# Modulation in two column halves, with six projection tiles begun between them

## The reference, cut to what matters

```python
c_act = silu(c)                                   # [1, 1024]
mod = c_act @ w_ada + b_ada                       # [1, 3072]
shift, scale, gate = split(mod, 3)
u = layer_norm(x) * (1 + scale) + shift           # [512, 1024]
proj = u @ w_in + b_in                            # [512, 12288]
a_v, a_g, b_b, b_c, b_h, b_g, c_a, c_b, c_g, merge = split(proj, ...)
... # pooling (a), short convolution (b), 31-tap convolution of c_a * sigmoid(c_b) (c)
m = sum over i of sigmoid(merge_i) * (y_i @ w_branch[i])
x = layer_norm(ALPHA * x + gate * (m @ w_out), ln_g, ln_b)
... # second block: two layers of attention, gates and a feed-forward part
```

## Time and profile before

| | |
|---|---|
| median of three runs | 2192.2 us |
| the profiled execution's own time | 2193.3 us |
| its span | 2191.5 us |
| TensorE busy | 2162.6 us, 99% |
| VectorE busy | 1258.1 us, 57% |
| ScalarE busy | 770.9 us, 35% |
| granted TensorE clock, mean | 0.996 |

### The profile page before, as it was taken

How to read it: one execution, slowest core, us unless ns; L and a number is a source line. 1 busy time by engine, 2 the same in 40 slices (tenths; PEclk the granted TensorE clock), 3 DMA queues, 4 the chain that set the end, 5 groups by cost and what they waited for, 6 DMA issues and landing times.

```text
span 2191.5 us, 25652 instructions
## 1 busy us (share of the span) xinstructions
PE 2162.6 (99%) x10739; PEld 1798.8 (82%) x10739; DVE 1258.1 (57%) x1617; ACT 770.9 (35%) x1019; POOL 24.9 (1%) x42
## 2 busy tenths in 40 slices
PE   6999999999999999999999999999999999999998
PEld 3888888888888888988888888889898888888887
DVE  7899797944656847434765554234743476555422
ACT  2323232323343354344353333135434434333311
POOL 1000000000000100000000000000000000000000
PEclk9999999999999999999999999999999999999999
DMA  9432232332233322322223233222232222323322
GB/s 318 137 116 82 96 101 82 99 112 96 96 101 101 103 71 77 111 77 78 96 77 99 94 105 103 91 78 89 76 114 77 77 96 78 98 95 102 107 90 77
DMA packets 184151, 217.90 MB, mean 99 GB/s; under 512 B 3805, under 2 KB 159077, under 8 KB 184037
## 3 DMA queue, kind: packets, MB, share of 16 engines
q1 hardware_dynamic: 180048, 210.52, 28.8%
q10 hardware_dynamic: 3252, 3.60, 0.5%
q0 software_dynamic: 736, 2.15, 0.3%
HBM read 212.06 MB, written 4.19 MB: 99 GB/s over the span
## 4 chain that ended last, share of the span: by engine, by line
PE 95%; DVE 1%; SPq 1%; ACT 1%; DMA 1%; issue 0%; POOL 0%; POOLq 0%; ACTq 0%; DVEq 0%
PE psum L1684 30%; PE psum L1686 30%; PE psum L1685 30%; PE psum L1974 1%; SPq L609 1%; PE psum L2005 1%; PE psum L2037 1%; DMA raw<-in_w_in 1%; PE psum L2017 1%; DVE hT L1385 0%; DVE whl L498 0%; PE psum L1961 0%; PE psum L1990 0%; ACT hT L825 0%; PE psum L1708 0%
## 5 line engine op out<-in xcount | busy, mean ns | idle before, releaser
L1684 PE MATMUL psum<-hT,whl 128*128 128x512 f32 (+1 forms) x2112 | 803.0, 380 | 7.0 <-DVE hT L1385 3.6
L1685 PE MATMUL psum<-hT,whl 128*128 128x512 f32 (+1 forms) x2112 | 796.5, 377 | 0.0
L1686 PE MATMUL psum<-hT,whl 128*128 128x512 f32 (+1 forms) x2112 | 796.4, 377 | 0.0
L498 DVE TENSOR_TENSOR whl<-raw,whl 128x1024 fp32r<-128x1024 f32 (+1 forms) x364 | 442.1, 1216 | 447.9 <-ACT whl L491 447.7
L491 ACT ACTIVATE whl<-raw 128x1024 fp32r<-128x1024 f32 (+1 forms) x364 | 380.0, 1047 | 447.3 <-PE psum L1686 429.2
L1684 PEld LDWEIGHTS psum<-hT,whl 128*128 128x128 f32 x2112 | 398.7, 189 | 87.7 <-issue 9.6
L1686 PEld LDWEIGHTS psum<-hT,whl 128*128 128x128 f32 x2112 | 398.7, 189 | 73.6
L1685 PEld LDWEIGHTS psum<-hT,whl 128*128 128x128 f32 x2112 | 399.0, 189 | 71.5 <-issue 0.5
L1684 PE MATMUL psum<-whl,ff 128*128 128x512 f32 x352 | 137.1, 390 | 0.0
L1686 PE MATMUL psum<-whl,ff 128*128 128x512 f32 x352 | 136.9, 389 | 0.0
L1685 PE MATMUL psum<-whl,ff 128*128 128x512 f32 x352 | 136.9, 389 | 0.0
(11 more groups left out here) (285 smaller groups left out, 2140.2 us busy)
## 6 DMA issues: line engine op xcount, KB each, us to landing
raw<-in_w_in SPq DMA_DIRECT2D x88, 1024.0 KB, 5.0
raw<-in_w_up SPq DMA_DIRECT2D x44, 1024.0 KB, 5.0
raw<-in_w_down SPq DMA_DIRECT2D x20, 1024.0 KB, 5.0
ada<-in_w_ada SPq DMA_DIRECT2D x12, 1024.0 KB, 13.7
raw<-in_w_branch SPq DMA_DIRECT2D x12, 1024.0 KB, 5.2
raw<-in_w_out SPq DMA_DIRECT2D x12, 1024.0 KB, 5.0
x<-in_x SPq DMA_DIRECT2D x4, 512.0 KB, 6.1
v_by_token<-vnat ACTq DMA_DIRECT2D x4, 512.0 KB, 2.9
```

The lines of the kernel that those rows point to most:

```text
L498: nc.vector.tensor_tensor(whl_view(w, 1), raw_view(w), whl_view(w, 0).bitcast(F), ALU.subtract).then_inc(w_lo, 1)
L1684: M(out_, stat_hi, mov_hi, start=start, stop=False, **kw)
L1685: M(out_, stat_hi, mov_lo, start=False, stop=False, **kw)
L1686: return M(out_, stat_lo, mov_hi, start=False, stop=stop, **kw)
```

## The change

The modulation's blocks are worked through in the order 0, 2, 1, 3: blocks 0 and 2 give shift and scale of column blocks 0 to 3, blocks 1 and 3 those of 4 to 7. `modc` is formed in two halves (`s_mod` 1 and 2). After the first half the column blocks 0 to 3 are modulated and the first six tiles (CA, CB, CG) run over contraction steps 0 to 3; between these partial tiles TensorE does the products of blocks 1 and 3; after the second half come column blocks 4 to 7 and the tiles' other four steps. Six weight tiles must lie split at once, so tiles 4 and 5 get room in the part of `ada` that block 0 has left (`room_for` waits for `s_mod` 1 there). The loads follow the new order, and the gate columns are loaded in one go after `s_mod` 2, ahead of chunk 5. Statistics start with each row block of `x`, and the normalised rows are written by ScalarE, for which VectorE prepares minus mean times the inverse deviation (`nmr`). Tiles of the first block use PSUM banks shifted by four; transposed columns use banks 0 to 3, 7, 6, 7, 6. The gate sums and the rest of the pair loops keep their places; `split_lo` and `split_hi` of tiles 3 to 5 have moved ahead of them.

```diff
-    PE_ROWS = (3, 3, 3, 5)
+    MOD_ORDER = (0, 2, 1, 3)
+    PE_ROWS = {0: 3, 2: 5, 1: 3, 3: 3}
+    X_BANK = (0, 1, 2, 3, 7, 6, 7, 6)
-            W_BANK[key] = count % 6
+            W_BANK[key] = (count + 4) % 6
+    apart.update({i: over(f"early{i}", at_ * K, [P, 2, 1024], R) for i, at_ in ((4, 0), (5, 8))})
 # room_for
+            elif w in (4, 5):
+                nc.scalar.wait_ge(s_mod, 1)
 # SP
-            for q in range(8):
-                ...
-            chunk_load(0)
-            chunk_load(1)
-            for q in range(4):
-                if q == 0:
-                    sp.wait_ge(s_mod, 1)
-                sp.dma_start(ada[:, q, :]..., wa[:, :, 2048 + q * 256:...]).then_inc(s_adag, 16)
-                chunk_load(2 + q)
-            for c in range(6, len(chunks)):
+            ada_load(0)          # two pieces each
+            ada_load(2)
+            chunk_load(0)
+            chunk_load(1)
+            ada_load(1)
+            chunk_load(2)
+            ada_load(3)
+            chunk_load(3)
+            chunk_load(4)
+            sp.wait_ge(s_mod, 2)
+            for q in range(4):
+                sp.dma_start(ada[:, 2 + q, :]..., wa[:, :, 2048 + q * 256:...]).then_inc(s_adag, 16)
+            for c in range(5, len(chunks)):
 # ScalarE
+            for tb in range(TB):
+                act.wait_ge(s_nmr, tb + 1)
+                A(xn1[:, tb, :], x[:, tb, :], ACT.Identity, bias=nmr[...], scale=rstd[...]).then_inc(s_xn, 1)
             split_hi(0)
-            split_hi(1)
-            act.dma_start(cstage[:], ...)
-            act.dma_start(gaterow, ...)
             act.wait_ge(s_modc, 1)
-            for ct in range(KT):
-                ...
+            columns_hi(0)
+            columns_hi(1)
+            split_hi(1)
+            columns_hi(2)
+            columns_hi(3)
+            for w in range(2, 6):
+                split_hi(w)
+            act.wait_ge(s_modc, 2)
+            columns_hi(4)
+            act.dma_start(cstage[:], ...)
+            act.dma_start(gaterow, ...)
+            for ct in range(5, KT):
+                columns_hi(ct)
 # VectorE: the sums in MOD_ORDER, and
-            for ct in range(0, KT, 2):
-                ...
+            ada_sum(0)
+            ada_sum(1)
+            modulation(0)
+            u_whole(0)
+            u_lo(0)
+            split_lo(0)
+            u_lo(1)
+            split_lo(1)
+            u_whole(2)
+            u_lo(2)
+            u_lo(3)
+            split_lo(2)
+            split_lo(3)
+            ada_sum(2)
+            split_lo(4)
+            split_lo(5)
+            ada_sum(3)
+            modulation(1)
+            for ct in range(4, KT, 2):
+                u_whole(ct)
+                u_lo(ct)
+                u_lo(ct + 1)
 # pair loops, ScalarE and VectorE (split_hi and split_lo alike)
-                    split_lo(W[key] + 3)
+                    if W[key] >= 3:
+                        split_lo(W[key] + 3)
 # TensorE, behind the vector transposes; part_tile(i, ks) is tile i of the first six over steps ks
             ada_product(1)
-            ...
+            take(6)
+            ada_columns(0)
+            ada_columns(1).then_inc(s_mod, 1)
+            for ct in range(4):
+                x_columns(ct)
+            part_tile(0, [0])
+            part_tile(0, [1])
+            part_tile(1, [0, 1])
+            part_tile(0, [2])
+            part_tile(1, [2])
+            part_tile(0, [3])
+            part_tile(1, [3])
+            ada_product(2)
+            part_tile(2, range(4))
+            part_tile(3, range(4))
+            ada_product(3)
+            ada_columns(2)
+            part_tile(4, range(4))
+            ada_columns(3).then_inc(s_mod, 1)
+            x_columns(4)
+            pe.wait_ge(s_modc, 2)
+            x_columns(5)
+            part_tile(5, range(4))
+            x_columns(6)
+            part_tile(0, [4])
+            x_columns(7)
+            part_tile(0, [5])
+            part_tile(1, [4])
+            part_tile(0, [6])
+            part_tile(1, [5])
+            part_tile(0, [7])
+            part_tile(1, [6, 7])
+            for i in range(2, 6):
+                part_tile(i, range(4, KT))
```

More of the change, by code:

```diff
@@ L355, in build @@
     bnst, mv, ssq, msq, rstd, neghalf = stat[:, 0:48], stat[:, 48:56], stat[:, 56:60], stat[:, 60:64], stat[:, 64:68], stat[:, 68:72]
-    modc, cact = stat[:, 72:88], stat[:, 88:96]
+    modc, cact, nmr = stat[:, 72:88], stat[:, 88:96], stat[:, 96:100]
     nmax, den = (stat[:, o_:o_ + 32].rearrange("p (k b h) -> p k b h", k=2, b=TB) for o_ in (0, 72))
@@ L371, in build @@
         w_hi, w_lo, w_used = sem("w_hi"), sem("w_lo"), sem("w_used")
-        s_x, s_vec, s_vec2, s_cst, s_cst2, s_adag, s_bcast = (sem(n) for n in ("x_in", "vec_in", "vec2_in", "cst_in", "cst2_in", "adag_in", "bcast_in"))
+        s_x = [sem(f"x_in{tb}") for tb in range(TB)]
+        s_vec, s_vec2, s_cst, s_cst2, s_adag, s_bcast = (sem(n) for n in ("vec_in", "vec2_in", "cst_in", "cst2_in", "adag_in", "bcast_in"))
         s_ada = [sem(f"ada_in{q}") for q in range(8)]
         s_c, s_cT, u_act = sem("c_in"), sem("c_transposed"), sem("u_by_act")
-        arow_ps, s_part = sem("ada_row_psum"), sem("ada_part")
+        arow_ps, s_part, s_nmr, s_xc = sem("ada_row_psum"), sem("ada_part"), sem("neg_mean_rstd"), sem("x_columns")
         s_vT, s_vcol, s_mod, s_modc, s_gp, s_gate = (sem(n) for n in ("vecT", "vcol_ready", "mod_psum", "modc_ready", "gate_psum", "gate_ready"))
@@ L670, in _ @@
             A(cact, bank(7)[:, 496:504], ACT.Silu).then_inc(s_cact, 1)
+            for tb in range(TB):
+                act.wait_ge(s_nmr, tb + 1)
+                A(xn1[:, tb, :], x[:, tb, :], ACT.Identity, bias=nmr[:, tb:tb + 1], scale=rstd[:, tb:tb + 1]).then_inc(s_xn, 1)
             act.wait_ge(s_vT, 6)
@@ L687, in _ @@
                         act.wait_ge(h_lo, ct - 1)
[L688 to L691, removed]
+                    A(utmp[:, 1, :], bank(X_BANK[ct]), ACT.Identity, bias=modc[:, ct:ct + 1], scale=modc[:, 8 + ct:9 + ct]).then_inc(u_act, 1)
+                A(hT[:, 0, ct, :], bank(X_BANK[ct]), ACT.Identity, bias=modc[:, ct:ct + 1], scale=modc[:, 8 + ct:9 + ct]).then_inc(h_hi, 1)
+            act.wait_ge(s_modc, 1)
+            columns_hi(0)
[7 more added lines that the diff above has]
+            columns_hi(4)
+            act.dma_start(cstage[:], t["consts"][:, NKEEP:NCONST]).then_inc(s_cst2, 16)
+            act.dma_start(gaterow, t["b_ada"][:, 2048:3072].to_broadcast((P, D))).then_inc(s_bcast, 16)
+            for ct in range(5, KT):
+                columns_hi(ct)
             def pair_step(p, key, j):
@@ L729, in _ @@
                     w = W[key]
-                    split_hi(w + 3)
+                    if w >= 3:
+                        split_hi(w + 3)
                     j = key[1] % 2
@@ L1054, in row_stats, with neg_mean_rstd @@
                 V.tensor_scalar(msq[:, tb:tb + 1], mv[:, 2 * tb + 1:2 * tb + 2], LN_EPS, None, ALU.add).then_inc(s_ms, 1)
-            dve.wait_ge(s_x, 16 * TB)
+            def neg_mean_rstd(tb):
+                dve.wait_ge(s_rstd, tb + 1)
+                V.tensor_scalar(nmr[:, tb:tb + 1], mv[:, 2 * tb:2 * tb + 1], rstd[:, tb:tb + 1], -1.0, ALU.mult, ALU.mult).then_inc(s_nmr, 1)
             for tb in range(TB):
+                dve.wait_ge(s_x[tb], 16)
                 half_stats(tb, 0)
@@ L1060, in _ @@
                 row_stats(tb)
[L1061 to L1064, removed]
+                if tb:
+                    neg_mean_rstd(tb - 1)
+            neg_mean_rstd(TB - 1)
             def weighted(o_, at_k, ks=range(KT)):
@@ L1075, in summed, with ada_sum @@
             def summed(g):
-                return weighted(adsum[:, 2 * g:2 * g + 2, :], lambda k: ada[:, 2 * g:2 * g + 2, k * 256:(k + 1) * 256])
+                return weighted(adsum[:, 2 * g:2 * g + 2, :], lambda k: ada[:, 2 + 2 * g:4 + 2 * g, k * 256:(k + 1) * 256])
             dve.wait_ge(s_cact, 1)
-            for b in range(TB):
+            def ada_sum(i):
+                b = MOD_ORDER[i]
                 if PE_ROWS[b] < 4:
@@ L1084, in _, with modulation @@
                 weighted(part, lambda k: ada_rows(b, k), range(PE_ROWS[b], KT)).then_inc(s_part, 1)
-                dve.wait_ge(s_part, b + 1)
-                dve.wait_ge(arow_ps, b + 1)
+                dve.wait_ge(s_part, i + 1)
+                dve.wait_ge(arow_ps, i + 1)
                 own = part[32 * b:32 * b + 1, :]
                 V.tensor_tensor(own, own, bank(7)[32 * b:32 * b + 1, :], ALU.add).then_inc(s_adsum, 1)
[L1090 to L1094, removed]
+            def modulation(h):
+                halves = lambda ap: ap.rearrange("p (a b) -> p a b", a=2)[:, :, 4 * h:4 * h + 4]
+                dve.wait_ge(s_mod, h + 1)
+                link(V.tensor_tensor(halves(modc), halves(vcol[:, VOFF["b_ada"]:VOFF["b_ada"] + 16]), halves(bank(6)[:, 0:16]), ALU.subtract))
```

(37 more changed lines are left out.)

27 lines of the change are left out of this document (12 added, 15 removed).

## The result

The changed kernel took 2200.43 us (median; 2199.13 to 2200.74), the kernel before 2192.62 in the same series: a ratio of 1.0034, 95% interval 1.0024 to 1.0045. It is 7.8 us slower, by the interval 5.3 to 9.9; the forecast was 9.1 slower, 2201.3.

What follows compares the result with a forecast made beforehand. TensorE, busy 99% of the span, was taken as the bound, with VectorE's list to the gate sum deciding this case: 6.9 us later plus 2.2 for the clock, 9.1 slower, 2201.3 us; range 2195.5 to 2206.

Steps and rivals of the forecast that it cites:

- The start: Up to tile 2: first projection at 30.35 us instead of 40.44, 5.3 us at half clock, tile 2 done at 66.9.
- the 2.8 us to spare: Block 3's modulation sum complete at 49.9 us, while TensorE wants it at 52.7.
- No gain from ten early microseconds: At tile 2 TensorE has done 36 steps at 66.9 us instead of 68.0, only 1.1 us ahead.
- What is late next: VectorE's list from tile 2 to the second gate sum ends at 99.0, 6.9 us later; TensorE waits 7.7 us.
- The clock behind the wait: After TensorE's wait for the gate sum the clock falls to half speed, costing 1.7 to 2.65 us, taken as 2.2.
- The 4.6: Price of half clock after the gate wait by the Trainium skill's reckoning, idle time counted; total loss then 11.5 us.
- The sum: Whole kernel: 6.9 us for the later gate sum plus 2.2 for the clock, 9.1 us slower.
- the two cases that it adds up: Range's upper end, 2206 us: late block 3 (2204.3 at 3 us) together with a longer half clock after the gap.
- The first (VectorE does not bind): Gate sum not binding, only the earlier start counts: 2191.1 us, or 2189 with full clock at the start; 13%.
- The full-clock start: No half clock at the first projections: tile 2 at 64.85, total 2199.2 us; 12%.
- Block 3's delay: Block 3's load, queued behind chunk 2's wait on SP, comes late and delays tile 2; 2204.3 us at 3 us; 10%.
- The longer half clock: After the gate wait the clock stays low longer, costing 4.6 us instead of 2.2: 2203.7 us; 8%.

Runs made afterwards that it cites:

- experiment 1: Changed kernel with 15 convolution items of VectorE, behind tiles CB, CB and CG of pair 0, handed out later in that pair: 2191.91 us, ratio 0.9994.
- experiment 9: Kernel before with only six idle matmuls added in TensorE's wait near 756 us: 2191.78 us, ratio 0.9996.
- experiment 6: Kernel before with 15 convolution items of pair 0 handed out later in the same pair: 2192.94 us, ratio 1.0001.
- experiment 2: Changed kernel with the gate product and VectorE's step reading it moved from behind the first AG tile to behind the first BC tile: 2198.47 us.
- experiment 5: Kernel before, start untouched, with ten convolution items of pair 0 moved ahead of the gate sums: 2201.26 us, ratio 1.0037.
- experiment 3: Changed kernel with eight idle matmuls in front of the gate product's wait: 2198.41 us, ratio 1.0026.
- experiment 4: Changed kernel with three idle matmuls between the first four column transposes and the first projection step: 2200.68 us, ratio 1.0034.

## Why the prediction was right

- *The start.* `modc` was forecast at 26.5 and came at 26.68, the first step at 30.35 and came at 30.52. The half-clock stretch was taken as 5.3 us of work and was 3.4 (31.3 to 34.7); the block 3 pieces landed 1.8 later than worked out (44.37), inside the 2.8 us to spare. Tile 2 still came at 66.87, forecast 66.9. That it fits so closely is luck: the 24 early matmuls were through 0.5 us sooner than worked out, the list behind them took 0.2 longer, and ScalarE's read came 0.3 after TensorE had gone on to the next tile; and with the same new start tile 2 came between 65.73 and 67.09 in the traces of the experiments.
- *No gain from ten early microseconds.* The 36 steps done at 66.87 would be done at 68.0 in the old order. With the later wait removed (experiment 1) the next pair was 0.7 us ahead, where 1.1 was forecast. One pair of executions does not show this, though: with the old start the same read came at 161.48 in experiment 9 and at 162.81 in experiment 6, so 161.58 lies inside the spread, and the 1.1 is neither shown nor refuted.
- *What is late next.* The second sum came at 98.99 (forecast 99.0), TensorE's wait was 7.8 (7.7). Experiments 1, 2, 5 and 6 show that this list is the cause: take work out of it and the loss goes, move its consumer and the wait moves, make it late in the kernel before and the loss comes, shorten it there and nothing happens.
- *The clock behind the wait.* 2.2 was taken, 1.93 read in the trace, 1.91 shown by experiment 3; the traces of experiments 4 and 5 have 1.45 and 2.50, so 2.2 lies in the middle of what single executions gave. The 4.6 that the prediction gives for counting the idle part too has no working there; half of the 6.8 us measured is 3.4.
- *The sum.* 9.1 forecast; 8.83 in the trace behind the first pair; 7.8 between the medians. Between the two profiled executions the difference is 7.3, and there the missing 1.6 is a half-clock stretch near 1760 that the kernel before had and the changed one had not, no step of the change. That the same makes the 1.0 between 8.83 and the medians is not shown, as only one execution of each was traced. The range's upper end, 2206, should be 2206.7 by the two cases that it adds up.
- *The rivals.* The first (VectorE does not bind) fell with the 7.8 us of waiting. The full-clock start is real but a matter of the execution, 1.07 instead of the 2.05 worked out. Block 3's delay was there and covered. The longer half clock did not come: 3.9 us with work, where it needed some nine.

Not shown: what the new load order does alone, whether experiment 1's 0.6 us are a gain, and what sets its two groups of runs apart.

## What to carry to other kernels

When a start is made earlier, find the next instruction that a second engine must feed, and carry that engine's list forward from the event that opens it: here the opening event, tile 2's end, moved 7 us later although the first matmul moved 10 us earlier. A list that just fits (0.2 us of waiting) is a deadline, and no busy share shows it. Work in the list that nobody waits for goes behind the deadline, before the event that opens the list is moved.

## What the runs showed of the hardware

The same start, instruction for instruction, met the clock differently in different executions: 0.50 from 31.3 to 34.7 in the changed kernel, no fall in experiment 3, a fall before 27.4 in experiment 4, ahead of the matmuls that were added. Tile 2 moved by 1.07 us with it. With the old start untouched, tile 2 was read between 58.99 and 60.31 us in four traces. The Trainium skill (TensorE: Matmul & The Clock Gate, What's actually happening) says of a kernel's start that the number of slow matmuls is "run-variable". The traces show the like behind a pause: about eight slow ones in the changed kernel's first steps, none in experiment 3's. A difference of a microsecond or two between single profiled executions of this kernel is therefore not a cause by itself: the stage near 1760 alone gave 1.6. Where runs fall into groups, as in experiments 1 to 3, a median alone does not show one either; a distance inside one trace, as from one CB read to the next, does.
